# The norm between two stages: sample columns and one weight split on GpSimd, the second reciprocal amid the first half, the third tile's first chunks in one piece

## The reference, cut to what matters

```python
def rmsnorm(x, g):
    y = xf * lax.rsqrt(jnp.mean(xf * xf, axis=-1, keepdims=True) + EPS)
    return (y * g.astype(jnp.float32)).astype(x.dtype)

def modulate(x, g, shift, scale):
    return rmsnorm(x, g) * (1 + scale[:, None, :]) + shift[:, None, :]

x = x + m[:, 2][:, None, :] * y              # end of a stage
h = modulate(x, norm_g[l, 1], m[:, 3], m[:, 4])
x = x + m[:, 5][:, None, :] * swiglu(h, ffn_w_up[l], ffn_w_down[l])
```

## Time and profile before

| | us |
|---|---|
| median of 3 runs (1617.2 to 1623.3) | 1619.62 |
| the profiled execution | 1624.05 |
| its span | 1622.4 |
| PE busy, share of the span | 95% |
| DVE busy | 67% |
| ACT busy | 48% |
| POOL busy | 12% |
| TensorE's granted clock | 0.989 |

### The profile page before, as it was taken

The page is one execution under the profiler, slowest core; times in us unless marked ns, Lnnn a source line. Parts: engine busy times, 40 slices in busy tenths (PEclk is TensorE's granted clock), DMA queues, the critical chain, the costliest instruction groups (busy, mean ns, idle before and its releaser), DMA issues.

```text
span 1622.4 us, 34774 instructions
## 1 busy us (share of the span) xinstructions
PE 1547.6 (95%) x13929; PEld 1405.5 (87%) x13929; DVE 1092.2 (67%) x2242; ACT 783.1 (48%) x1655; POOL 196.0 (12%) x334
## 2 busy tenths in 40 slices
PE   5999989999999999989999999999999999999997
PEld 3899769899999999989999655555889999999996
DVE  5799956966757657674272467676468586875866
ACT  4567764643525525443223556565355353452544
POOL 2001320000000000312000355334000000000000
PEclk9999999999999999999999999999999999999998
DMA  9899642244556645454232500210421422332321
GB/s 320 264 296 299 173 135 79 78 154 140 164 166 208 197 147 185 138 153 118 59 79 90 142 27 2 53 31 25 118 65 53 117 79 77 103 91 86 102 79 59
DMA packets 238205, 200.68 MB, mean 124 GB/s; under 512 B 8210, under 2 KB 196962, under 8 KB 237776
## 3 DMA queue, kind: packets, MB, share of 16 engines
q1 hardware_dynamic: 230768, 174.61, 36.1%
q0 software_dynamic: 6976, 23.78, 5.1%
q10 hardware_dynamic: 304, 0.10, 0.0%
HBM read 188.87 MB, written 11.20 MB: 123 GB/s over the span
## 4 chain that ended last, share of the span: by engine, by line
PE 79%; DVE 8%; ACT 5%; issue 4%; DMA 1%; POOL 1%; DVEq 0%; ACTq 0%; POOLq 0%
PE ps L2342 32%; PE ps L2674 26%; PE ps L2322 5%; PE ps L2393 4%; PE ps L2358 2%; PE ps L2799 2%; PE ps L2846 2%; PE ps L2727 2%; PE ps L2539 1%; DVE t L1598 1%; POOL Pp L882 1%; DVE wl L1530 1%; ACT Hh L999 1%; DMA ada<-in_w_ada_dram 1%; PE ps L2873 1%
## 5 line engine op out<-in xcount | busy, mean ns | idle before, releaser
L919 ACT ACTIVATE wh<-raw 128x1024 fp32r<-128x1024 f32 (+2 forms) x129 | 118.5, 922 | 273.6 <-PE ps L2342 254.8
L2674 PE MATMUL ps<-Hh,bh 128*128 128x288 f32 x608 | 180.5, 297 | 1.0 <-DVE t L2006 1.0
L2674 PE MATMUL ps<-Hh,bl 128*128 128x288 f32 x608 | 179.0, 294 | 0.0
L2674 PE MATMUL ps<-Hl,bh 128*128 128x288 f32 x608 | 179.0, 294 | 0.0
L2342 PE MATMUL ps<-Hh,wh 128*128 128x288 f32 (+1 forms) x688 | 151.8, 302 | 3.5 <-ACT u_s L1097 2.0
L2342 PE MATMUL ps<-Hh,wl 128*128 128x288 f32 (+1 forms) x688 | 148.2, 297 | 0.0
L2342 PE MATMUL ps<-Hl,wh 128*128 128x288 f32 (+1 forms) x688 | 147.8, 297 | 0.0
L1530 DVE TENSOR_TENSOR wl<-raw,wh 128x1024 fp32r<-128x1024 f32 (+2 forms) x129 | 135.8, 1054 | 15.4 <-ACT wh L919 14.8
L2342 PE MATMUL ps<-ah,wh 128*128 128x288 f32 x656 | 140.9, 297 | 0.8 <-issue 0.8
L2342 PE MATMUL ps<-al,wh 128*128 128x288 f32 x656 | 140.5, 296 | 0.0
L2342 PE MATMUL ps<-ah,wl 128*128 128x288 f32 x656 | 140.5, 296 | 0.0
(11 more groups left out here) (395 smaller groups left out, 3903.1 us busy)
## 6 DMA issues: line engine op xcount, KB each, us to landing
ada<-in_w_ada_dram SPq DMA_DIRECT2D x64, 1024.0 KB, 8.3
raw<-in_ffn_w_up_dram SPq DMA_DIRECT2D x88, 512.0 KB, 4.9
raw<-in_conv_w_pw_dram SPq DMA_DIRECT2D x24, 512.0 KB, 9.3
raw<-in_ffn_w_down_dram SPq DMA_DIRECT2D x32, 384.0 KB, 3.4
raw<-in_ffn_w_down_dram SPq DMA_DIRECT2D x32, 320.0 KB, 3.0
raw<-in_w_kv_dram SPq DMA_DIRECT2D x12, 512.0 KB, 4.6
out_win_sample_dram<-in_state_win_dram POOLq DMA_DIRECT2D x8, 512.0 KB, 4.8
C<-in_cache_kv_dram POOLq DMA_DIRECT2D x32, 128.0 KB, 3.9
```

The costliest lines, as they stand in the source:

```text
L919: A(wh[:, u % RING, 0:K, 0:w], raw[:, u % RING, 0:K, 0:w], ACT.Copy).then_inc(hi_ready, 1)
L2674: last = M(ps[:, bank, 0:HT], wt[:, blk, k], rt, start=(j in (0, 1, 2, 6) and k == 0 and i == 0), stop=(k == 3 and i == 2), skip_group_che ...
```

## The change

At boundaries 0 to 2, and not at boundary 3:

- GpSimd gets a function `sample_norm(g)`: it splits one weight (the third unit's of `first_three`, 128x1024), and norms the samples' columns (three instructions of 128x512). DVE no longer does these four.
- DVE runs the first two `scaled` straight behind the first reciprocal, ahead of `residual_hi` and of the other weight split; both `residual_hi` follow `low` of chunk 1; the second reciprocal stands behind `low` of chunk 4 and no longer behind the whole first half.
- ACT rounds the third unit's weight after `high` of chunk 1 (before: of chunk 3), takes both second-half squares before chunk 3, the second root after chunk 4, and loads the Silu table (L1047, boundaries 0 and 2) amid the first half.
- TensorE sums the first half's squares before chunk 3 of `last_pair` (before: 4). In `first_three` the third unit's first half joins at chunk 5: its chunks 0 to 4 in one piece, then chunk by chunk with the other two. It no longer waits for the second half of the next-to-last tile of the stage before it starts, only for the first.

```diff
+            def sample_norm(g):
+                u, k = end_unit(g) + 1 + SPLIT_AHEAD, HALF_NORM[g]
+                sh = NORMS[k][1]
+                pool.wait_ge(hi_ready, u + 1)
+                pool.wait_ge(lo_ready, u)
+                nc.gpsimd.tensor_tensor(wl[:, u % RING], raw[:, u % RING], wh[:, u % RING].bitcast(F32),
+                                        ALU.subtract).then_inc(lo_ready, 1)
+                f4 = fs[:].rearrange("p c (b t) -> p c b t", b=NB)
+                pool.wait_ge(S("n_a"), g + 3 + (k > 3))
+                pool.wait_ge(x_upd, DC * (HALF_RES[g] + 1))
+                nc.gpsimd.tensor_tensor(f4, x[:, :, TP:T].rearrange("p c (b t) -> p c b t", b=NB),
+                                        acoef[:, :, 1:].unsqueeze(3).to_broadcast([P, DC, NB, NT]), ALU.mult).then_inc(S("n_s"), 1)
+                pool.wait_ge(S("st_r"), 2 * g + 3)
+                pool.wait_ge(S("n_s"), 3 * g + 1)
+                nc.gpsimd.tensor_tensor(fs[:], fs[:], r[:, TP:T].unsqueeze(1).to_broadcast([P, DC, TS]),
+                                        ALU.mult).then_inc(S("n_s"), 1)
+                pool.wait_ge(S("n_s"), 3 * g + 2)
+                nc.gpsimd.tensor_tensor(f4, f4, mods[:, sh * DC:(sh + 1) * DC, 1:].unsqueeze(3).to_broadcast([P, DC, NB, NT]),
+                                        ALU.add).then_inc(S("n_s"), 1)
...
@@ ACT, end_stage, behind the first root @@
                 split_hi(u + SPLIT_AHEAD)
+                if g < 3:
+                    high_half(0, 0)
+                    high_half(0, 1)
+                    split_hi(u + 1 + SPLIT_AHEAD)
+                    high_half(0, 2)
+                    square_half(g, DC - 2, 1)
+                    square_half(g, DC - 1, 1)
+                    high_half(0, 3)
+                    high_half(0, 4)
+                    root_half(g, 1)
...
@@ DVE, end_stage, behind the first reciprocal @@
+                if g < 3:
+                    dve.wait_ge(S("st_r"), 2 * g + 2)
+                    scaled(0, 0)
+                    scaled(0, 1)
+                    split_lo(u + SPLIT_AHEAD)
+                    low(0, 0)
...
+                    inverse_half(g, 1)
+                    scaled(0, 6)
...
@@ PE, first_three @@
-                pe.wait_ge(tile_free, u0 + 2 - RING)
+                pe.wait_ge(tile_free, u0 + 1 - RING)
+                pe.wait_ge(S("x_half"), 2 * g + 1)
                 for k in range(DC):
                     if k == 3:
                         stat_half(g, 1)
+                    elif k == THIRD_AT:
+                        pe.wait_ge(lo_ready, u0 + 3)
+                        pe.wait_ge(S("x_half"), 2 * g + 2)
+                        for behind in range(k):
+                            block_of(u0 + 2, behind, 0, Hh, Hl, DC)
                     pe.wait_ge(S("n_lo"), 17 * g + k + 1)
-                    for u in (u0, u0 + 1):
+                    for u in (u0, u0 + 1, u0 + 2)[:3 if k >= THIRD_AT else 2]:
                         block_of(u, k, 0, Hh, Hl, DC)
```

More of the change, by code:

```diff
@@ L99 @@
 STEPS = (CW + 3) // 4
+THIRD_AT = 5
 RING = 3
@@ L818, in through @@
                                    a["state_win"][n - 1].rearrange("s t h d -> s (t h d)")).then_inc(S("thru"), 16)
+            sample_norm(0)
             pool.wait_ge(S("cr_out"), 16 * (1 + NT))
@@ L838, in _ @@
             pool.dma_start(w1v[:], w1[1]).then_inc(S("pe_in"), 16)
-            for b in range(2, NB):
+            pages(2)
+            sample_norm(1)
+            for b in range(3, NB):
                 pages(b)
@@ L889, in _ @@
                                                 ALU.mult).then_inc(S("s_scaled"), 1)
+            sample_norm(2)
             f4 = xf[:, :, TP:T].rearrange("p c (b t) -> p c b t", b=NB)
@@ L1028, in end_stage @@
                 split_hi(u + SPLIT_AHEAD)
+                if g < 3:
[8 more added lines that the diff above has]
+                    root_half(g, 1)
+                    if keeps:
+                        act.wait_ge(S("st_tb"), g + 2 + (g + 1) // 2)
+                        A(scrap[:], epst[:], ACT.Silu).then_inc(S("st_tb"), 1)
+                    for cc in range(5, DC):
+                        high_half(0, cc)
+                    act.wait_ge(S("n_s"), 3 * g + 3)
+                    A(Hh[:, :, TP:T], fs[:], ACT.Copy).then_inc(S("n_hi"), 1)
+                    if keeps:
+                        act.wait_ge(tile_done, u + 2)
+                        A(Tf[1][:, :, TP - HT:], fs[:, 4:8], ACT.Copy).then_inc(S("t_whole"), 1)
+                    for cc in range(DC):
+                        high_half(1, cc)
+                    return
                 square_half(g, DC - 2, 1)
@@ L1039, in end_stage @@
                 high_half(0, 7)
[L1040 to L1052, removed]
+                for tb in range(2):
+                    act.wait_ge(S("f_pe"), tb + 1)
+                    A(stage[:, tb].rearrange("p (b f) -> p b f", b=2), ps[:, 2 * tb:2 * tb + 2, :], ACT.Copy).then_inc(S("fe_act"), 1)
                 for cc in range(DC):
@@ L1613, in end_stage @@
                 inverse_half(g, 0)
+                if g < 3:
[4 more added lines that the diff above has]
+                    low(0, 0)
+                    scaled(0, 2)
+                    low(0, 1)
+                    residual_hi(g, DC - 2)
+                    residual_hi(g, DC - 1)
+                    scaled(0, 3)
+                    low(0, 2)
+                    add_half(g, 1)
+                    scaled(0, 4)
+                    low(0, 3)
+                    scaled(0, 5)
+                    low(0, 4)
+                    inverse_half(g, 1)
+                    scaled(0, 6)
+                    low(0, 5)
+                    scaled(0, 7)
+                    low(0, 6)
+                    low(0, 7)
+                    dve.wait_ge(S("st_r"), 2 * g + 3)
+                    scaled(1, 0)
+                    scaled(1, 1)
+                    dve.wait_ge(S("n_hi"), 17 * g + 9)
+                    V.tensor_tensor(Hl[:, :, TP:T], fs[:], Hh[:, :, TP:T].bitcast(F32), ALU.subtract).then_inc(S("n_lo"), 1)
+                    for cc in range(DC):
+                        low(1, cc)
+                        if cc + 2 < DC:
+                            scaled(1, cc + 2)
+                    dve.wait_ge(lo_ready, u + 2 + SPLIT_AHEAD)
+                    return
                 residual_hi(g, DC - 2)
@@ L2405, in last_pair @@
                         for k in range(K):
-                            if h == 1 and u == u0 and k == 4:
+                            if h == 1 and u == u0 and k == 3:
                                 stat_half(g, 0)
```

15 lines of the change are left out of this document (removed).

## The result

The changed kernel takes 1625.91 us in the median of 20 runs, the kernel before 1620.97 (20 runs beside it). One of the changed kernel's runs, of 6011.66 us, is far off the others and stands outside the ratio: 1.0025, 95% interval 1.0016 to 1.0034, which is +4.1 us (2.6 to 5.5). By the bound of 0.5% that is no change, on the slow side. A second series gave 1.0021 (1.0007 to 1.0035). The forecast was +2.4 us.

What follows compares the result with a forecast made beforehand. DVE was taken to set the pace at the boundaries, TensorE waiting 11.1 us for `low`. Boundary sums +0.54, +1.33 and +0.54 us, together +2.4, gave 1622.0 us against the median; own range 1618 to 1627, 8 in 10 1610 to 1627.

Steps and rivals of the forecast that it cites:

- gone from DVE's chain: DVE at boundaries 0 to 2: earlier first reciprocal, four instructions less, fewer waits; -4.21 us at 0 and 2, -3.59 at 1.
- held by the split: DVE's two-operand instruction waits while GpSimd splits the weight: 2.02 us at boundaries 0 and 2, 2.19 at 1.
- held by the samples' three: GpSimd's three samples instructions delay DVE's `scaled` and `low` at each boundary, by 2.73 us, as at boundary 3.
- wait for the second root, beyond the 0.41: DVE before its second reciprocal: 0.41 us counted because the root comes later than DVE is ready, nothing more.
- rival (a): At boundaries 0 to 2 GpSimd's instructions run beside DVE's at no cost: -11.5 us, 1608.1; chance 0.15.
- DVE is held: At boundaries 0 to 2, two-operand DVE instructions and GpSimd's SBUF reads go one after the other; the forecast's sign hangs on it.
- rival (c): GpSimd's split into the rounded format is dear, at four times DVE's 1.22, 4.9 us: +10.4 us, 1630.0; chance 0.06.
- Rival (b): Partial cover at the boundaries: GpSimd slips into DVE's waits and reciprocal, half of 14.4 us saved: -4.8 us, 1614.8; chance 0.11.
- The prediction's sign for the stretch: DVE, first reciprocal to first second-half `low`: 20.5 to 21 us would show the forecast right, 16 us rival (a).
- TensorE's wait moves: TensorE in `first_three`: earlier start shortens one wait, but chunk 2 comes late, so the wait only shifts; counted at nothing.
- The third unit's piece, at nothing: TensorE at chunk 5: runs 2.0 us of the third unit's blocks while waiting; gains only where TensorE ends last, so nothing.

Runs made afterwards that it cites:

- the four runs: Changed kernel with GpSimd only writing: memsets in place of its four instructions, split and samples' norm left out; ratio 0.9910 (0.9894 to 0.9926).
- the last experiment: Third unit joins at chunk 7, not 5, against the version with the split beside the second reciprocal and samples on DVE; ratio 1.0008 (0.9997 to 1.0018).

## Why the prediction was right, and the step that was mis-sized

The forecast, no measurable change, +2.4 us, held: +4.1 us, inside its own range. In part this is luck: 2.4 us that the forecast had at nothing were half made up by 1.2 us that it had too much, and no change within 0.5% leaves 8.1 us to either side. Its terms, forecast and measured (us, boundaries 0, 1, 2):

| | forecast | measured |
|---|---|---|
| gone from DVE's chain | -4.21, -3.59, -4.21 | taken over |
| held by the split | 2.02, 2.19, 2.02 | 1.71, 2.15, 1.67 |
| held by the samples' three | 2.73 each | 2.56, 2.56, 2.58 |
| wait for the second root, beyond the 0.41 | 0 | 0.04, 1.74, 0.66 |
| sum | +0.54, +1.33, +0.54 | +0.10, +2.86, +0.70 |
| by the stretches, less 0.40 | | +0.13, +2.89, +0.72 |

"Held" is the stretched duration less that of the same instruction alone (1.93 - 0.22, 2.67 - 0.52; 1.33, 1.54 and 1.22 less 0.51 each). "Taken over" means that the forecast's own figure stands in the sum. The sum, 3.66 us, meets the stretches' 3.74 and the 3.86 from reciprocal to reciprocal.

- **What leaves DVE's chain.** Right. With all four back on DVE the stretches were 17.9 for the expected 18.0; with GpSimd's cost taken out they were 16.26, 15.89 and 15.89, where the forecast has 19.63 - 4.21 + 0.40 = 15.82 (boundary 0) and 15.82 (1). The 0.4 us more at boundary 0 are what rival (a) allowed for: the second root is waited for 0.81 us there and 0.44 at the other two. The first reciprocal did move by a block: TensorE's first wait at boundary 1 begins 2.63 us behind its start before and 3.03 behind it after. Rival (a)'s sum of -11.5 us was the right size for its case by the stages, 11.4; the four runs say 14.6, at least 12.0.
- **DVE is held.** Right, and in size within 0.35 us each. The split in the rounded format took 2.35 to 2.49 us for the estimated 2.38, so rival (c) fell. Rival (b), half the cost, fell with the measured 4.2 to 4.7 us held at every boundary. The prediction's sign for the stretch, 20.5 to 21 us, was met only at boundary 2: boundary 0 came out below, boundary 1 above.
- The Trainium skill ("SBUF — State Buffer", Who interferes with whom) says that a DVE instruction with two SBUF inputs contends with a GpSimd instruction that reads SBUF, not with one that only writes, and that one with at most one SBUF input, outside the two-port performance modes, does not contend. Three runs agree on the three parts: 2.67 us beside the split, 0.52 beside the memset, and the reciprocal's 1.95 beside the split.
- **"TensorE's wait moves", at nothing.** This is the step that failed, in size. The prediction saw that chunk 2 would come late, but counted only which engine ends last, and a TensorE that waits was taken to lose nothing else. At boundary 1 it waits 1.62 and 2.01 us with six matmuls between, at boundary 2 3.55 in one piece, and runs at 1.2 GHz behind, just where the sum of squares stands on which DVE's next reciprocal hangs. That is 1.74 + 0.66 us, and with idle matmuls in those waits it was gone: 0.45 us of waiting at all three. With the split's and the samples' over-estimate (0.7 and 0.5 us) against it, +2.4 became +3.7.
- **The third unit's piece, at nothing.** Not tested in the changed kernel, where DVE ends last. With DVE relieved, its place at chunk 5 and not 7 is worth 5.8 us at the three boundaries, as the last experiment shows.

What stays open is when the lower clock comes. Before the change TensorE waits 2.72 us at boundary 1 and stays at 1.00; with the samples alone on GpSimd it waits 1.62 and 1.87 at boundary 1 without a drop and 1.87 at boundary 2 with one. The length of the waits alone does not decide it.

## What to carry to other kernels

In these runs work that reads SBUF, moved from DVE to GpSimd, cost DVE next to nothing only beside instructions with at most one SBUF operand (a reciprocal here). Place it there, by a semaphore if need be: the same split cost 2.15 us in one place and 0.37 in another. Then look at who waits for its result, for the later start cost TensorE 1.5 us at each boundary, and doing the split on DVE was only 0.7 us slower in all. Where such a move makes an engine's waits longer, look at what TensorE has to do next behind them: a few matmuls that release the next step are bad ones to run at 1.2 GHz (1.65 us at boundary 1).

## What the runs showed of the hardware that was not expected

- TensorE at half pace behind waits of only 1.6 and 2.0 us (granted clock 0.62 and 0.64 in 717 to 726 us), in both profiles of the changed kernel; 32 idle matmuls in the waits of boundary 1 keep it at 1.00, and 1.65 us are won there.
- Two executions of one kernel differ in a stage that no change touches: in the attention, 1008 to 1021 us, the granted clock is 0.62 in the first profile of the changed kernel (0.61 before) and 1.00 in its second, and from the reciprocal of boundary 1 to that of boundary 2 they take 487.54 and 481.64 us. In the twelve profiles the clock of this stretch is anything from 0.61 to 1.00. A difference of a few us between two spans has to be read stage by stage before it is put down to the change; how much of it stands in a difference of medians no run shows.
